# Delta rule: two token tiles of the last gate chunk are multiplied in the chain's stage, ahead of the blocks of the inverse

## The reference, cut to what matters

```python
proj = h @ w_in
qkv = causal_depthwise_conv_silu(proj[..., :o1], conv_w)
z = proj[..., o1:o2].reshape(b_sz, t_len, GDN_HEADS, GDN_DV)
...
sol = lax.linalg.triangular_solve(a_strict, rhs, left_side=True, lower=True, unit_diagonal=True)
...
def step(state, inp):
    qg, kd, u_i, w_i, a_i, gl = inp
    v_new = u_i - jnp.einsum("bhcd,bhde->bhce", w_i, state)
    o = jnp.einsum("bhcd,bhde->bhce", qg, state) + jnp.einsum("bhcs,bhse->bhce", a_i, v_new)
    state = state * gl[..., None, None] + jnp.einsum("bhcd,bhce->bhde", kd, v_new)
    return state, o
...
o = rms_norm(o, out_norm) * jax.nn.silu(z)
return o.reshape(b_sz, t_len, GDN_V_WIDTH) @ w_out
```

## Time and profile before

| | |
|---|---|
| median of 3 runs | 2214.41 us (2212.40 to 2216.28) |
| the profiled execution | 2214.89 us, its span 2213.1 us |
| TensorE busy (PE) | 2147.5 us, 97% of the span |
| VectorE busy (DVE) | 1147.4 us, 52% |
| ScalarE busy (ACT) | 816.9 us, 37% |
| mean granted clock of TensorE | 0.987 of 2.4 GHz |

### The profile page before, as it was taken

The page is one execution under the profiler, slowest core; times in us unless marked ns, Lnnn a source line. Parts: engine busy times, 40 slices in busy tenths (PEclk is TensorE's granted clock), DMA queues, the critical chain, the costliest instruction groups (busy, mean ns, idle before and its releaser), DMA issues. The chain is left out here.

```text
span 2213.1 us, 26090 instructions
## 1 busy us (share of the span) xinstructions
PE 2147.5 (97%) x10710; PEld 1702.4 (77%) x10710; DVE 1147.4 (52%) x1706; ACT 816.9 (37%) x1169; POOL 38.5 (2%) x34
## 2 busy tenths in 40 slices
PE   8999999999999999999999999999999889999998
PEld 6776678888888877778877888887786577888886
DVE  5674765442542579887836444324623736444423
ACT  4324753331232455542533222213315734322212
POOL 0120000000000000000100000000000000000000
PEclk9999999999999999998999999999999999999999
DMA  4220013222223222343122222222240031222221
GB/s 172 85 84 31 1 58 105 96 95 95 87 89 105 81 82 95 108 125 82 40 95 68 91 92 94 94 95 95 96 166 26 1 115 60 93 96 95 95 96 67
DMA packets 43111, 190.68 MB, mean 86 GB/s; under 512 B 15520, under 2 KB 16224, under 8 KB 22384
## 3 DMA queue, kind: packets, MB, share of 16 engines
q1 hardware_dynamic: 40656, 184.78, 24.6%
q10 hardware_dynamic: 2336, 4.23, 0.6%
HBM read 185.25 MB, written 3.74 MB: 85 GB/s over the span
## 5 line engine op out<-in xcount | busy, mean ns | idle before, releaser
L250 DVE TENSOR_TENSOR weights_low<-weights_raw,weights_high 128x2048 fp32r<-128x2048 f32 (+1 forms) x161 | 365.5, 2270 | 591.3 <-ACT weights_high L223 591.2
L440 PE MATMUL psum<-split,weights_high 128*128 128x512 f32 x1448 | 574.7, 397 | 8.2 <-PEq L146 4.5
L441 PE MATMUL psum<-split,weights_high 128*128 128x512 f32 x1448 | 573.2, 396 | 0.0
L442 PE MATMUL psum<-split,weights_low 128*128 128x512 f32 x1448 | 571.3, 395 | 0.0
L223 ACT CAST weights_high<-weights_raw 128x2048 fp32r<-128x2048 f32 (+1 forms) x161 | 304.0, 1888 | 575.3 <-PE psum L442 532.6
L440 PEld LDWEIGHTS psum<-split,weights_high 128*128 128x128 f32 x1448 | 271.5, 188 | 78.7 <-issue 7.1
L442 PEld LDWEIGHTS psum<-split,weights_low 128*128 128x128 f32 x1448 | 271.5, 188 | 65.7
L441 PEld LDWEIGHTS psum<-split,weights_high 128*128 128x128 f32 x1448 | 271.6, 188 | 64.0
L441 PE MATMUL psum<-hidden_low,weights_high 128*128 128x512 f32 x256 | 102.1, 399 | 0.0
L440 PE MATMUL psum<-hidden_high,weights_high 128*128 128x512 f32 x256 | 100.9, 394 | 0.0
L442 PE MATMUL psum<-hidden_high,weights_low 128*128 128x512 f32 x256 | 100.4, 392 | 0.0
(11 more groups left out here) (485 smaller groups left out, 3103.3 us busy)
## 6 DMA issues: line engine op xcount, KB each, us to landing
weights_raw<-in_weights SPq DMA_DIRECT2D x161, 1024.0 KB, 4.8
minus_c<-minus_c_rows ACTq DMA_DIRECT2D x16, 256.0 KB, 7.1
x_stream<-in_x SPq DMA_DIRECT2D x4, 512.0 KB, 7.0
gdn_in_grown<-gdn_rows SPq DMA_DIRECT2D x4, 512.0 KB, 4.6
chain_grown<-gdn_rows SPq DMA_DIRECT2D x4, 512.0 KB, 3.7
out<-end_results SPq DMA_DIRECT2D x8, 256.0 KB, 2.1
table<-rope_tables SPq DMA_DIRECT2D x1, 1024.0 KB, 12.4
weights_raw<-in_weights SPq DMA_DIRECT2D x1, 768.0 KB, 4.1
```

The source lines that it names most:

```text
L250: self.nc.vector.tensor_tensor(out=self.low_of(n)[:, 0:width], in0=self.raw[:, n % 2, 0:width], in1=self.high_of(n)[:, 0:width].bitcast(se ...
L440: nc.tensor.matmul(bank, wh, ah, start=first, stop=False)
L441: nc.tensor.matmul(bank, wh, al, start=False, stop=False)
L442: return nc.tensor.matmul(bank, wl, ah, start=False, stop=last)
```

## The change

Of the last gate chunk, only the first two token tiles are still multiplied in the projection's stage. The class `LateGates` multiplies the other two (24 matmuls) and evicts them (two Tanh on ScalarE, four operations on VectorE) in the chain's stage. TensorE does this first, before `level5_first(0)`; ScalarE does it ahead of its first copy; VectorE does it after `keys(0)` and `values(0)`, before the three copies. The partial sums of the first three chunks' features stay in banks 7 and 5 over the barrier. The chain takes the banks in the order 0, 1, 2, 3, 4, 6, 5, 7, and the first job in bank 5 or 7 waits until both late tiles have been read.

In the right side the two halves of the features change places, so that the last chunk needs feature tiles 0 to 3 of `split`. The two buffers of `kd` also change places. With both, the late matmuls read other memory than the chain's first `kd` and the query-key product are written to. Two waits on `closed` (the late tiles' last step) are added: on ScalarE ahead of the first Exp into `growth`, which lies over the buffer of the gates' products, and on VectorE ahead of the gating of tiles 2 and 3.

```diff
@@ -327,7 +327,7 @@
 decay = cols(gdn, DT, 2 * GH, fixed(GDN_QKV + D), 1)
-gates = [halves(gdn, T, fixed(GDN_QKV + T * side), half) for side in range(2) for half in range(2)]
+gates = [halves(gdn, T, fixed(GDN_QKV + T * side), half) for side in range(2) for half in (side, 1 - side)]
 return features[:1] + [decay] + features[1:] + gates
@@ -2101,6 +2101,44 @@
+LATE = 2
+class LateGates:
+    def __init__(self, chunk, token_split, z2, spare, gate_done, banks):
+        self.chunk, self.split, self.z2, self.gate_done, self.banks = chunk, token_split, z2, gate_done, banks
+        self.mixed, self.tanh = spare[:, 0:2, :], spare[:, 2:4, :]
+        self.gain = place("gate_gain", 153, [P, P])
+        self.tokens = tuple(range(TT - LATE, TT))
+    def signals(self, s):
+        self.tanh_ready, self.read, self.closed = [s.sem("late_gate_" + n) for n in ("tanh_ready", "read", "closed")]
+    def tensor(self, pe):
+        parts = weights.parts(Chunk(self.chunk), 4)
+        for j in self.tokens:
+            for k in range(4):
+                token = [self.split[:, n, k, j * P:(j + 1) * P] for n in range(2)]
+                last = product(psum[:, self.banks[j], :], token, [p[:, k, :] for p in parts], False, k == 3)
+            last.then_inc(weights.products, 1)
+    def scalar(self, act):
+        for i, j in enumerate(self.tokens):
+            act.wait_ge(weights.products, self.gate_done(1, j))
+            nc.scalar.activation(self.tanh[:, i, :], psum[:, self.banks[j], :], ACT.Tanh, scale=0.5).then_inc(self.tanh_ready, 1)
+    def vector(self, dve):
+        for i, j in enumerate(self.tokens):
+            dve.wait_ge(self.tanh_ready, i + 1)
+            nc.vector.scalar_tensor_tensor(out=self.mixed[:, i, :].rearrange("p (h c) -> p h c", h=4),
+                                           in0=psum[:, self.banks[j], :].rearrange("p (h c) -> p h c", h=4), scalar=0.5,
+                                           in1=self.gain[:].unsqueeze(1).broadcast_to([P, 4, P]),
+                                           op0=ALU.mult, op1=ALU.mult).then_inc(self.read, 1)
+            dve.wait_ge(self.read, i + 1)
+            nc.vector.scalar_tensor_tensor(out=self.z2[:, j, T:2 * T], in0=self.tanh[:, i, :], scalar=1.0,
+                                           in1=self.mixed[:, i, :], op0=ALU.add, op1=ALU.mult).then_inc(self.closed, 1)
 def gdn_project(ahead_of, split, qkv, z2, lower, columns, scratch, kept, spare, inverses):
@@ -2121,10 +2159,12 @@
+    late_gates = LateGates(z_chunk + 3, split, z2, spare, gate_done, (4, 6, 7, 5))
     def bank_of(o):
...
-    gate_banks = ((3, 0, 1, 2), (4, 6, 7, 5))
+    gate_banks = ((3, 0, 1, 2), late_gates.banks)
     highs_behind, lows_behind = [
@@ -2134,7 +2174,7 @@
         masks = s.sbuf("masks", [P, 2, P], f32)
-        gate_gain = place("gate_gain", 153, [P, P])
+        gate_gain = late_gates.gain
         selector, log_floor = place("sum_selector", 153.5, [P, 64]), place("log_floor", 153.75, [P, 2])
@@ -2310,12 +2350,13 @@
                 for side in range(2):
-                    for half in range(2):
-                        chunk = z_chunk + 2 * side + half
+                    for turn in range(2):
+                        half = turn if side == 0 else 1 - turn
+                        chunk = z_chunk + 2 * side + turn
                         pe.wait_ge(weights.low_ready, chunk + 1)
                         parts = weights.parts(Chunk(chunk), 4)
-                        for j in range(TT):
-                            if half == 0:
+                        for j in range(TT if (side, turn) != (1, 1) else TT - LATE):
+                            if turn == 0:
                                 if side == 0:
@@ -2324,11 +2365,12 @@
                                 token = [split[:, n, a, j * P:(j + 1) * P] for n in range(2)]
-                                last = product(psum[:, gate_banks[side][j], :], token, [p[:, k, :] for p in parts], a == 0, a == DT - 1)
+                                last = product(psum[:, gate_banks[side][j], :], token, [p[:, k, :] for p in parts],
+                                               turn == 0 and k == 0, turn == 1 and k == 3)
                             last.then_inc(weights.products, 1)
-                            if side == half == 0 and j == 1:
+                            if side == turn == 0 and j == 1:
                                 turn_logs(1)
-                        if side == half == 0:
+                        if side == turn == 0:
                             pe.wait_ge(col_dve, 12)
@@ -2389,7 +2431,7 @@
                     weights.split_high(act, Chunk(z_chunk + 2 + 2 * side))
-                    for j in range(TT):
+                    for j in range(TT if side == 0 else TT - LATE):
                         o = n_tiles + TT * side + j
@@ -2570,10 +2612,13 @@
+    return late_gates
 class GdnChain:
...
-    def __init__(self, s, qkv, z2, lower, columns, kept, spare, inverses, split):
+    def __init__(self, s, qkv, z2, lower, columns, kept, spare, inverses, split, late_gates):
+        late_gates.signals(s)
         NH = TT * GH
@@ -2605,8 +2650,11 @@
+        bank_order = (0, 1, 2, 3, 4, 6, 5, 7)
+        late_banks = [late_gates.banks[j] for j in late_gates.tokens]
         def bank(job):
-            return job_of[job] % 8
+            return bank_order[job_of[job] % 8]
@@ -2624,8 +2672,10 @@
                     pe.wait_ge(*released[number - 8])
+                if bank_order[number % 8] in late_banks and number < 8:
+                    pe.wait_ge(late_gates.read, LATE)
                 job_of[job], released[number] = number, release
-                return number % 8
+                return bank_order[number % 8]
@@ -2723,7 +2773,7 @@
                     for i, h in enumerate(half_heads[half]):
-                        last = nc.tensor.matmul(psum[:, b, i * P:(i + 1) * P], kd[:, n % 2, h, :], vn[:, 0, h, :], start=True, stop=True)
+                        last = nc.tensor.matmul(psum[:, b, i * P:(i + 1) * P], kd[:, (n + 1) % 2, h, :], vn[:, 0, h, :], start=True, stop=True)
                     last.then_inc(done, 1)
@@ -2750,6 +2800,7 @@
                 take(job, (kd_ready if job[0] == "kt" else bv_ready, job[2] + 1))
+            late_gates.tensor(pe)
             level5_first(0)
@@ -2807,6 +2858,8 @@
                         act.wait_ge(qg_ready, n - 1)
+                    else:
+                        act.wait_ge(late_gates.closed, LATE)
                     nc.scalar.activation(growth[:], grown[:], ACT.Exp).then_inc(growth_ready, 1)
@@ -2862,6 +2915,7 @@
+            late_gates.scalar(act)
             first_copy(0)
@@ -2900,7 +2954,7 @@
                         wait_job(dve, ("ds", n - 2, half))
-                    nc.vector.tensor_tensor(out=kd[:, n % 2, 4 * half:4 * half + 4, :], in0=result(("kt", n, half)),
+                    nc.vector.tensor_tensor(out=kd[:, (n + 1) % 2, 4 * half:4 * half + 4, :], in0=result(("kt", n, half)),
                                             in1=column(e_key, n, half), op=ALU.mult).then_inc(kd_ready, 1)
@@ -2979,6 +3033,8 @@
                 dve.wait_ge(inverted, n + 1)
+                if n in late_gates.tokens:
+                    dve.wait_ge(late_gates.closed, LATE)
                 for half in range(2):
@@ -3014,6 +3070,7 @@
             values(0)
+            late_gates.vector(dve)
             level5(0)
@@ -3045,7 +3102,7 @@
             for number in range(len(job_of) - 8, len(job_of)):
-                if number % 8 == b:
+                if bank_order[number % 8] == b:
                     pe.wait_ge(*released[number])
@@ -3285,7 +3342,7 @@
 minus_c_in = enter(nc.semaphore("minus_c_loaded"))
-gdn_project(ahead_of, split, qkv, z2, lower, columns, scratch, kept, spare, (inverse, inverse_t))
+late_gates = gdn_project(ahead_of, split, qkv, z2, lower, columns, scratch, kept, spare, (inverse, inverse_t))
@@ -3313,7 +3370,7 @@
     ffn_entry = feed_forward_entry(s, 0)
-    chain = GdnChain(s, qkv, z2, lower, columns, kept, spare, (inverse, inverse_t), gdn_out_split)
+    chain = GdnChain(s, qkv, z2, lower, columns, kept, spare, (inverse, inverse_t), gdn_out_split, late_gates)
     mix_out = projection(s, "gdn_out", 0, ffn_entry, gdn_out_split, chain)
```

## The result

The changed kernel takes 2217.73 us (median of 20 runs, 2214.40 to 2222.29), the kernel before 2214.47 us (2211.29 to 2219.21). The ratio is 1.0016, with a 95% interval of 1.001 to 1.0021. That is 3.3 us more. The profiled execution of the changed kernel took 2219.78 us, its span 2218.0 us; it lies 2 us over the median, that of before 0.5 us over its own. A second series of the changed kernel (e12) gave 2218.51 us and a ratio of 1.0023 (1.0013 to 1.0033). Two executions far outside all others, one of the kernel before beside e9 to e12 (5905.91 us) and one of e11 (2651.66 us), are left out of the ratios and move no median given here by more than 0.15 us.

The account below looks back on a forecast made before the run. TensorE, busy 97% of the span, was taken as the bound. Terms 2.15 + 0.2 + 1.5 - 0.7 = +3.15 us gave 2218.04 us for a profiled execution, 2217.6 us against the median; range 2210 to 2222.5.

Parts of the forecast that it names:

- rival A: First token tile's blocks: late products carry full clock through them, so faster, 2210.1 to 2211.6 us; chance 0.18.
- Part 1: Old stage without 24 matmuls: VectorE sets its end, chain starts 3.47 us earlier, TensorE's pause grows to 3.78 us.
- Rival C: Old stage's end: barrier waits for something other than VectorE, chain up to 1.6 us later, 2219.2 us; chance 0.09.
- Part 2: In front of the blocks: 24 matmuls take 5.62 us at full clock, first block starts 2.15 us later.
- Part 3: Moved evictions and new waits at the blocks: the third job waits for its bank's read, +0.2 us (0 to 0.7).
- Part 4: TensorE's clock on the 24 late matmuls: the first ones slow after the pause, +1.5 us (0 to 5.1).
- Part 5: Clock in the blocks: the fall comes anyway, a little later, -0.7 us (-6.7 to +3).
- the terms outside the clock: Later first block (2.15 us) plus evictions and new waits at the blocks (0.2 us): +2.35 us.
- those of the clock: Slow first late products after the pause (+1.5 us) and the saving in the blocks (-0.7 us).
- Rival B: Slow clock in both places: all late products slow (5.1 us), nothing saved behind, 2221.2 us; chance 0.20.
- rival D: Clock moves nowhere: no fall after the 3.78 us pause, slow stretch as before, 2216.8 us; chance 0.08.

Follow-up runs that it names:

- e12: The changed kernel again, unchanged, for a second profile; 2218.51 us, ratio 1.0023.
- e9: e1 again, unchanged, run side by side with e10; 2214.01 us, ratio 1.0002.
- e11: e4 with 3 of the 24 late products put back in the old stage, in front of the transposes; 2208.27 us, ratio 0.9979.
- e1: Changed kernel with VectorE's low part of the next chunk moved from the old stage to behind the chain's first-tile values; 2215.79 us, ratio 1.0010.
- e6: e4 with all 24 late products together again in front of the first blocks; 2212.76 us, ratio 0.9994.
- e10: e6 again, unchanged, run side by side with e9; 2215.04 us, ratio 1.0005.
- e8: The kernel before, unchanged, for a second profile; one run, 2213.99 us.
- e5: e4 without the edit of e1, so late products spread but the long pause kept; 2210.22 us, ratio 0.9983.
- e4: e1 plus late products in three portions (12, 6, 6) before and between the blocks, late banks taking two bank-order turns; 2208.61 us, ratio 0.9974.
- e7: The kernel before with 24 useless 512-column products added in the places of e4's three portions; 2215.65 us, ratio 1.0004.
- e3: Changed kernel with one late token tile in place of two; 2214.60 us, ratio 1.0008.

## Why the prediction was right

The forecast was 2217.6 us, and the steps that carry it are what the runs show: the longer pause, slow late products (in one of two profiles), and a fall in the blocks that comes in any case. The clock is at 0.50 during the query-key products of the first token tile, which was the sign that decides against rival A. The sizes of the small terms are partly off, and one term had the wrong source.

**Part 1** held to 0.1 us. The chain's first product came 11.33 us behind the start of the last gate chunk; the prediction's 1020.77 is 11.41 us behind 1009.36. The pause was 3.69 us (3.78 forecast). e1 shows the cause: without VectorE's 2.28 us there, the stage ends 1.73 us earlier. Rival C is excluded by this, and by the 1.21 us between VectorE's end and the chain's start.

**Part 2** held. At full clock the late products take 5.79 us (e12), 0.17 more than 24 x 0.234, and the first blocks start 17.11 us behind the chunk's start against 14.88 before: 2.23 us later, where I had 2.15.

**Part 3** named the wait, but its price was not +0.2. The second blocks start 1.58 us behind the first, not 1.11. The trace names ScalarE's copy as the releaser (0.48 us), which now ends at 1031.35 + 0.77 = 1032.12. In e6 the late bank is not waited for, ScalarE does the same, and the second blocks follow 1.14 us behind the first (1025.82 and 1024.68). So it was the read of the late bank, whose end at 1031.36 + 0.69 = 1032.05 lies close to the copy's. The next step shows what it costs: the 64x64 blocks start 3.64 us behind the first blocks with this wait (the changed kernel and e1) and 3.43 without it (e6 and e10), so the wait itself is worth 0.2 us. Before, however, they start 3.76 us behind at full clock (e8), because VectorE is still at the values of the first tile when the first results of the second blocks are there. Against before, the step is 0.1 us shorter.

**Part 4** was right in size when it happens: 7.32 us, which is 1.70 over 5.62, with 1.5 forecast. But it does not happen in each execution. It did in the first profile and in e5, it did not in e12, all three with a pause of 3.7 us. Nor does the clock fall in the pause, as it did ahead of 1689.02: in the first profile the first three late products still run at a clock of 1.00, and the slow ones come behind them. The rule weighed there, that longer idle gaps between bursts of matmuls bring the slow clock back (the Trainium skill, TensorE: Matmul & The Clock Gate, section "Why this matters for your kernels"), agrees with two of the three.

**Part 5** was right that the fall comes in the blocks in spite of the large products in front; e4, e5 and e7 show that large products *between* the blocks keep it away (rival A named the wrong condition). The -0.7 us were read wrongly. I took them as what the slow clock costs in the second blocks, whose last result VectorE takes about 2.2 us behind their start at 1025.35. In e8 the same blocks run at full clock, and VectorE still takes the last result at 1027.58, 2.17 us behind their start at 1025.41: VectorE was busy with the values until 1026.7 and then made its three copies in a row, and the slow clock had no part in it. The gain in the first profile lies elsewhere and is larger: from the first 128x128 transposes (1036.16) to the second tile's 32x32 blocks (1046.97) it took 10.81 us, against 12.85 before and 12.56 in e8, because the clock came back sooner, before the new values and not behind them. How long the slow part lasts differs between executions of one kernel as well (17 and 13.6 us before), so two profiles of each kernel do not show that this gain is due to the change.

**The sum.** In the first profile the stretch grew by 1.55 us where I had 3.15, in e12 by 0.3 us over e8, and yet the medians moved by 3.3 and 4.5 us. The profiles compare executions with unequal clocks: over the stretch the mean is 0.76 and 0.81 before, but 0.82 and 0.86 in the changed kernel. The pair with nearly the same clock, e8 and the first profile of the changed kernel, differs by 37.36 - 35.20 = 2.16 us, which is the size of part 2, the longer pause. The same comparison can be made over all executions, by the mean granted clock of the whole execution (given to 0.001; in brackets the number of executions):

| mean granted clock | kernel before | changed kernel | difference |
|---|---|---|---|
| 0.985 | 2216.87 us (33) | 2220.47 us (7) | 3.60 |
| 0.986 | 2214.46 us (11) | 2218.52 us (8) | 4.06 |
| 0.987 | 2213.90 us (13) | 2217.82 us (10) | 3.92 |
| 0.989 | 2211.48 us (22) | 2214.64 us (5) | 3.16 |

At an equal clock the changed kernel is 3.2 to 4.1 us slower, and the clocks of the two hardly differ on the whole (0.9869 and 0.9865). So the loss is mostly not a matter of more slow time. The longer pause, 2.2 us, is the part that is shown; where the remaining 1 to 2 us lie stays open. In my sum the terms outside the clock made 2.35 us and those of the clock 0.8. The agreement of 2217.6 with 2217.73 is therefore in part luck. Rival B's picture (all late products slow) did not appear, while rival D's condition, a pause of 3.7 us without a fall, did in e12.

## What to carry to other kernels

Moving matmuls over a barrier helps only as far as the other engines can leave the old stage earlier. Look for the last engine at the join; here it was VectorE, so of the 5.6 us taken from TensorE only 3.5 came back as an earlier start of the chain, and the rest was a longer pause. When the clock falls in a run of small matmuls with waits between them, try large ones between them rather than in front: the same 24 products cost 3.3 us in front and gained 4.3 us in portions (e5). With VectorE's low part moved as well the gain was 5.2 us (e4), which is the fastest kernel of this case together with e11. And where an effect is a fifth of a percent, read it in the profile between two events near the change, take two profiles of the same kernel before believing either, and compare executions of equal granted clock.

## What the runs showed of the hardware that was not expected

Whether the clock falls behind a pause is not settled by the pause's length here. Of three profiles with 3.7 us two show a fall over the late products; of six with 1.9 to 2.2 us (e1, e3, e4, e6, e9, e10) two do, e9 and e10; of the five with 1.3 to 1.7 us none does before the first blocks. In all four cases the clock is still full in the pause itself and falls between 0 and 0.7 us after TensorE has begun again.

The same instructions gave stretches of 34.06 and 35.38 us (e1, e9), where the late products at 5.79 and 7.31 us make the difference, and of 32.42 and 35.28 us (e6, e10), where the late products (5.79 and 7.33 us) make half of it and a longer slow part in the blocks the other half.

With the blocks standing together all ten profiles show a fall in them, though TensorE is busy through the slow part (10.00 of 10.00 us in the changed kernel); with large products between them three of four show none, and the fourth (e11) one of 3.4 us. The large products did two things at once: they stood between the small blocks, and they filled the waits there (0.5 us and more). No run separates the two, so whether the small matmuls or the waits bring the clock down is not shown.
